# First feed-forward stage of a two-block transformer kernel: down projections of feature pairs by seven block products, conv taps of the gate by halves, values kept in the product banks

## The reference, cut to what matters

```
u = causal_depthwise_conv(h @ w_up, conv_w, conv_b)      # 3 taps along the positions
gate, val = split(u)                                     # 2816 columns each
y = (gelu(gate) * val) @ w_down
```

## Time and profile before

| | us |
|---|---|
| median of 3 runs | 2795.94 (2794.5 to 2797.42) |
| profiled execution | 2795.87 |
| its span, first to last instruction | 2794.1 |
| PE busy | 2703.7 (97%) |
| DVE busy | 1700.7 (61%) |
| POOL busy | 1650.8 (59%) |
| ACT busy | 906.3 (32%) |
| mean granted TensorE clock | 0.992 of full speed |

### The profile page before, as it was taken

How to read it: one execution, slowest core, us unless ns; L and a number is a source line. 1 busy time by engine, 2 the same in 40 slices (tenths; PEclk the granted TensorE clock), 3 DMA queues, 4 the chain that set the end, 5 groups by cost and what they waited for, 6 DMA issues and landing times.

```text
span 2794.1 us, 38419 instructions
## 1 busy us (share of the span) xinstructions
PE 2703.7 (97%) x13018; PEld 2160.0 (77%) x13018; DVE 1700.7 (61%) x2404; ACT 906.3 (32%) x1776; POOL 1650.8 (59%) x1253
## 2 busy tenths in 40 slices
PE   8999999898999999999999999989999999999998
PEld 5777777676878888887788887767787878888887
DVE  6666687738467777777734302475546356766667
ACT  5544444535211111114413113555233222122222
POOL 4555411455988777766533243212356998888874
PEclk9999999999999999999999999999999999999999
DMA  4322321034111211224411243212435111111134
GB/s 146 102 84 84 98 91 54 16 136 149 66 46 48 66 45 48 65 68 169 172 55 46 82 143 106 78 59 88 161 107 173 38 57 56 54 56 53 56 122 142
DMA packets 83012, 243.36 MB, mean 87 GB/s; under 512 B 7839, under 2 KB 11712, under 8 KB 82500
## 3 DMA queue, kind: packets, MB, share of 16 engines
q1 hardware_dynamic: 60800, 183.79, 20.7%
q10 hardware_dynamic: 22084, 57.86, 5.8%
HBM read 206.48 MB, written 32.52 MB: 86 GB/s over the span
## 4 chain that ended last, share of the span: by engine, by line
PE 80%; DVE 9%; POOL 5%; ACT 3%; issue 2%; DMA 0%; POOLq 0%; ACTq 0%; DVEq 0%; SPq 0%
PE ps L1069 14%; PE ps L1071 14%; PE ps L1070 14%; PE ps L1391 4%; PE ps L1392 3%; PE ps L1393 3%; PE ps L1443 3%; PE ps L1445 3%; PE ps L1444 3%; PE ps L1160 2%; PE ps L1483 2%; PE ps L1485 2%; PE ps L1484 2%; PE ps L1176 2%; POOL arena L868 1%
## 5 line engine op out<-in xcount | busy, mean ns | idle before, releaser
L800 POOL CAST wh<-raw 128x1024 fp32r<-128x1024 f32 x173 | 185.1, 1070 | 826.8 <-PE ps L1071 777.4
L1069 PE MATMUL ps<-hh,wh 128*128 128x512 f32 x1456 | 600.2, 412 | 15.5 <-DVE hl L2861 10.9
L1071 PE MATMUL ps<-hh,wl 128*128 128x512 f32 x1456 | 572.2, 393 | 0.0
L1070 PE MATMUL ps<-hl,wh 128*128 128x512 f32 x1456 | 571.5, 392 | 0.0
L802 POOL TENSOR_TENSOR wl<-raw,wh 128x1024 fp32r<-128x1024 f32 x173 | 417.9, 2416 | 13.9
L1069 PEld LDWEIGHTS ps<-hh,wh 128*128 128x128 f32 x1456 | 275.7, 189 | 87.6 <-issue 15.5
L1071 PEld LDWEIGHTS ps<-hh,wl 128*128 128x128 f32 x1456 | 275.4, 189 | 59.8
L1070 PEld LDWEIGHTS ps<-hl,wh 128*128 128x128 f32 x1456 | 276.2, 190 | 52.2 <-issue 3.4
L3154 DVE TENSOR_TENSOR arena<-ps,arena 128x512 f32<-128x512 f32 x288 | 195.8, 692 | 23.6 <-PE ps L1071 23.6
L894 POOL TENSOR_TENSOR wl<-raw,wh 128x512 fp32r<-128x512 f32 x136 | 189.7, 1394 | 10.9
L1069 PE MATMUL ps<-gated,wh 128*128 128x512 f32 (+1 forms) x464 | 178.9, 386 | 2.9 <-DVE gated L2952 2.6
(11 more groups left out here) (401 smaller groups left out, 5922.0 us busy)
## 6 DMA issues: line engine op xcount, KB each, us to landing
raw<-weights SPq DMA_DIRECT2D x226, 512.0 KB, 3.6
arena<-w_ada SPq DMA_DIRECT2D x48, 512.0 KB, 3.7
raw<-weights SPq DMA_DIRECT2D x88, 256.0 KB, 2.6
arena<-gate_scratch ACTq DMA_DIRECT2D x20, 512.0 KB, 4.3
arena<-x_t ACTq DMA_DIRECT2D x1, 4096.0 KB, 14.1
x_scratch<-arena ACTq DMA_DIRECT2D x2, 2048.0 KB, 8.9
arena<-x_scratch SPq DMA_DIRECT2D x2, 2048.0 KB, 9.7
gate_scratch<-arena ACTq DMA_DIRECT2D x16, 256.0 KB, 2.2
```

The source lines that it names most:

```text
L800: pool.tensor_copy(wh[:, s], raw[:, r]).then_inc(Z.wt_hi, 1)
L1069: pe.matmul(out, wh[:, slot, w], xh, start=start, stop=False)
L1070: pe.matmul(out, wh[:, slot, w], xl, start=False, stop=False)
L1071: return pe.matmul(out, wl[:, slot, w], xh, start=False, stop=stop)
```

## The change

The first stage gets the pair scheme of the second: `pair_up`, `pair_down`, `pair_unit`, `pair_loads`, `cast`, `first_blocks`, `second_blocks` and `pair_sums` take `use` as an argument, and the single-feature loops (`st_splits`, `st_chunks`, `st_step1`) go. The weights of the first stage are laid out in pairs too. New is the DVE and ACT order for a stage with a conv: the taps of gate go half by half, each half reading its own bank (the two columns that cross the halves are kept in a small copy, `EDGE`, and added by `edge_taps`); the value is convolved and multiplied half by half, half 1 first, and each product goes into bank 2 or 3. In the tail the down of the last pair takes the place of the single downs of feature 19. The diff's core:

```diff
@@ PE
-                st_up(0, 0)
-                st_down(0, 0)
-                if use == 0:
-                    st_up(1, 1)
-                    st_down(1, 1)
-                    with pe.Fori(0, (ST_N - 2) // 2) as i:
-                        for u in range(2):
-                            st_up(i * 2 + (2 + u), u)
-                            st_down(i * 2 + (2 + u), u)
-                    pe.sem_inc(Z.chunk_done, ST_CHUNKS)
+                st_up()
+                st_down()
+                pair_up(0, 1, 1, 1)
+                pair_up(1, 0, 2, 2)
+                pair_down(0, 3, 3)
+                pair_up(1, 1, 4, 4)
...
                 def pair_up(pair, second, k, ks):
+                    if use:
+                        pe.wait_ge(Z.g_lin, n * 2 + (ST_DONE - 1))
+                    else:
+                        pe.wait_ge(R.lin_first, gate_lin(n, 0))
+                        pe.wait_ge(Z.g_cv, gate_taps_done(n, 2 - 6))
+                    pair_block(k, ks, 0, 0, A_BLOCK[use][0, 0], True)
...
+                        pe.wait_ge(Z.g_cv, gate_taps_done(n, 4 - 6))
+                    pair_block(k, ks, 1, 1, S_BLOCK[use][2], True)
...
                     if second:
-                        pe.wait_ge(Z.a_hi, highs(pair, 1))
+                        pe.wait_ge(HIGH_SEM[use], highs(use, pair, 1))
                     else:
-                        pe.wait_ge(Z.a_lo, lows(pair, 6 - PAIR_LOWS))
-                    pair_block(k, ks, 3, 3, S_BLOCK[1][1], True)
+                        pe.wait_ge(LOW_SEM[use], lows(use, pair, 6 - PAIR_LOWS))
+                    pair_block(k, ks, 3, 3, S_BLOCK[use][1], True)
...
@@ PE, tail
                 half_tile(tail, 0, 0)
-                if use:
-                    pe.wait_ge(Z.a_lo, lows(PAIRS - 1, 8))
-                else:
-                    pe.wait_ge(val_free[0], NL * val_free[1])
+                pe.wait_ge(LOW_SEM[use], lows(use, PAIRS - 1, 8))
                 half_tile(tail, 0, 1)
...
-                if use:
-                    pair_down(PAIRS - 1, LAST_DOWN, LAST_DOWN)
-                    pe.sem_inc(Z.chunk_done, 2)
-                else:
-                    half_down(0, 0, range(KT))
+                pair_down(PAIRS - 1, LAST_DOWN, LAST_DOWN)
+                pe.sem_inc(Z.chunk_done, 2)
                 half_down(1, 0, low)
...
                 if use == 0:
-                    for features in (range(3), range(3, 4)):
-                        half_down(0, 1, features)
-                        half_down(1, 1, features)
+                    half_down(1, 1, low)
                     running_mean(5, 0)
                     half_down(2, 1, low)
-                    half_down(0, 1, high)
                     half_down(1, 1, high)
                     half_down(2, 1, high)
@@ ACT, one up of the new order (the first of a pair)
+            def first_up1(m, prev, k, ks):
+                before, n = prev * 2 + 1, m * 2
+                value_lin(before, 0)
+                gelu_half(before, 1)
+                pair_copy(0, n, k)
+                product_high(0, before, 1, A22_H, bank(3))
+                cast(0, k, ks, False, 2)
+                cast(0, k + 1, ks + 1, True, 0)
+                product_high(0, before, 2, A12_H, bank(2))
+                sum_high(0, prev, 4, S1_H, S1_F)
+                sum_high(0, prev, 5, S2_H, S2_F)
+                gate_first(n, k)
+                sum_high(0, prev, 7, S4_H, S4_F)
+                cast(0, k + 1, ks + 1, True, 1)
+                gelu_half(n, 0)
+                gate_second(n)
@@ DVE
+            def value_taps(n, half):
+                j, pair = n + ST_FIRST, bank(2, 2)
+                dve.wait_ge(Z.v_lin, n * 2 + (ST_FIRST + 2))
+                for m in range(2):
...
+                    dve.scalar_tensor_tensor(t, pair[:, a - 1 - m:end - 1 - m], conv_col(j, 5 - m), t, ALU.mult, ALU.add).then_inc(Z.v_cv, 1)
+            def gated_half(n, half):
+                t = half_of(half)
+                dve.wait_ge(Z.g_act, n * 2 + (ST_FIRST + 1 + half))
+                dve.wait_ge(Z.v_cv, value_taps_done(n, 2 if half else 4))
+                dve.tensor_tensor(bank(2 + half), ST_VALUE[:, t], ST_GATE[:, t], ALU.mult).then_inc(R.p_prod, 1)
+            def gated_value(n):
+                for half in (1, 0):
+                    value_taps(n, half)
+                    gated_half(n, half)
+            def pair_unit1(n, k, lows_left):
+                first_sums(0, n, k)
+                gate_taps(n, 0, 0)
+                gate_taps(n, 0, 1)
+                second_value(0, n, k)
+                if lows_left is not None:
+                    last_lows(0, lows_left)
+                second_gate(0, n, k)
+                gate_taps(n, 1, 0)
+                first_value(0, n, k)
+                gate_taps(n, 1, 1)
+                edge_taps(n)
+            def pair_step1(m, prev, k):
+                gated_value(prev * 2 + 1)
+                second_blocks(0, prev)
+                pair_unit1(m * 2, k, prev)
+                pair_sums(0, Y1t, prev, k + 1)
+                gated_value(m * 2)
+                first_blocks(0, m)
+                pair_unit1(m * 2 + 1, k + 2, None)
...
+            def last_lows(use, pair):
+                dve.wait_ge(LOW_SEM[use], lows(use, pair, 7))
+                block_low(use, pair, 7, S2_L, S2_F, S2_H)
+                block_low(use, pair, 8, S4_L, S4_F, S4_H)
...
             for u in range(2):
                 unit_taps(1, u, 0)
                 unit_taps(1, u, 1)
                 product1(1, u)
                 unit_low(1, u)
-            dve.wait_ge(Z.dn_free, 4 + 16 * ND)
+            pair_sums(0, Y1t, PAIRS - 1, LAST_DOWN)
```

More of the change, by code:

```diff
@@ L794, in _ @@
+            chunk_range(first, N_CHUNKS)
         @block.gpsimd
@@ L1310, in eight_tiles @@
                             ready(k)
-                        last = product(bank(y_bank(use, f, half)), c % SL, k, x[0][k][:, t], x[1][k][:, t], k == 0, k == KT - 1)
+                        last = product(bank(y_bank(use, f, half)), wt_slot(c), k, x[0][k][:, t], x[1][k][:, t], k == 0, k == KT - 1)
                         if n in (second, second + 3) and k == 3:
@@ L2718, in product_high @@
[L2718 to L2724 removed]
             def first_highs(pair, copy):
[L2727 removed]
+                product_high(1, pair * 2, 1, G1_F, bank(3))
@@ new lines, in first_blocks, with second_blocks @@
+            def first_blocks(use, pair):
+                dve.wait_ge(PROD_SEM[use], prods(use, pair * 2, 2))
+                dve.wait_ge(HIGH_SEM[use], highs(use, pair, 2))
+                block_sum(use, S3_F, 2, G1_F, ALU.subtract)
+                block_low(use, pair, 2, A11_L, bank(2), A11_H)
+                block_low(use, pair, 3, S3_L, S3_F, S3_H)
+            def second_blocks(use, pair):
+                dve.wait_ge(HIGH_SEM[use], highs(use, pair, 4))
+                block_sum(use, S1_F, 3, G1_F, ALU.add)
+                dve.wait_ge(LOW_SEM[use], lows(use, pair, 3))
+                block_sum(use, S2_F, 3, S3_F, ALU.subtract)
+                dve.wait_ge(PROD_SEM[use], prods(use, pair * 2 + 1, 2))
+                block_low(use, pair, 4, A22_L, bank(3), A22_H)
+                dve.wait_ge(HIGH_SEM[use], highs(use, pair, 5))
+                dve.wait_ge(LOW_SEM[use], lows(use, pair, 5))
+                block_sum(use, S4_F, 2, S2_F, ALU.subtract)
+                block_low(use, pair, 5, A12_L, bank(2), A12_H)
+                block_low(use, pair, 6, S1_L, S1_F, S1_H)
@@ L3608, in first_blocks @@
                 gate_half(n, 1)
+                first_value(1, n, k)
                 gate_half(n, 0)
[L3610 to L3635 removed]
@@ L3749, in chunks @@
     return w.reshape(k, P, feature_tiles, P).transpose(2, 1, 0, 3).reshape(feature_tiles, P, k * P)
-def ffn_chunks(gate, value, down):
-    out = 2 * [gate[0], value[0], gate[1], value[1]] + [down[0]]
-    for j in range(2, NL):
-        out += [gate[j], value[j], down[j - 1]]
-    a, b = NL, NL + 1
-    return np.stack(out + 2 * [gate[a], value[a], gate[b], value[b], down[ND], down[a], down[b]])
 def pair_chunks(gate, value, down):
```

947 lines of the change are left out of this document (478 added, 469 removed).

## The result

The changed kernel takes 2839.8 us (median of 4 runs, 2839.1 to 2842.19) against 2796.68 for the kernel before beside it: 1.0155 times as long, 95% interval 1.0137 to 1.0172. The prediction was 2811.5 with a range to 2827.0: the sign was right, the size, +15.6 for a measured +43, was not.

A forecast was written before the change was run, and what follows sets the result against it. PE was taken to set the time while DVE keeps its deadlines. Summed: -18.6 + 16.8 + 5.9 + 1.3 + 3.8 + 1.0 + 5.4 = +15.6 us on 2795.87, so 2811.5; 8 in 10 range 2788 to 2827.

The forecast's parts named there:

- Matmuls removed, with the pair's pace: First stage: 96 down matmuls fewer save 21.8 us, less 3.2 for the pairs' slower matmuls, leaving 18.6 us.
- Block 3's wait for A22_L: First up of each pair: PE waits for DVE's A22_L before block 3, 1.5 us in each of seven pairs.
- Second tile of the tail: Tail: PE waits for A12_L before the value's tile in bank 2, 5.9 us, bounds 4.4 and 8.
- First sum of the last down: Last pair's down: block 1 waits for a sum standing behind unit_low on DVE, 3.8 us.
- Half clock in the tail, over before: Tail: PE's clock drops after the last two stalls, costing 1.3 us for the longer and 1.0 for the shorter.
- Idle time given back later: Waits for the running mean and hl: 24 removed matmuls stood ahead of them, so 5.4 us return as idle time.
- two edge taps of about 0.20: DVE, each first-stage feature: the two taps across the halves cost about 0.20 us each.
- The products' port wait: DVE's gated products beside POOL: 0.5 us extra each, two before A22_L, so 1.0 us per pair; bounds 0 and 1.3 each.
- The second stall: Start of down: S2_L and S4_L make the first down sum late, 0.9 us in each of seven pairs, bounds 0.15 and 1.5.
- A: Rival: DVE is in time everywhere, all deadline stalls in loop and tail vanish, 2782.7 us; chance 0.15.
- B: Rival: no port waits, DVE's products fall between POOL's operations; -0.3 us, 2795.6 us; chance 0.20.
- C: Rival: full port waits on each product and low, 32.1 us in the loop; +33.0, 2828.9 us; chance 0.12.

The follow-up runs named there:

- e0: Changed kernel with each feature's two edge taps left out, semaphore counts kept (two gate columns lack terms): 2812.7 us, 1.0052 of the kernel before.
- e12: Changed kernel with the two edge taps written as three one-column DVE operations, nothing left out: 2816.9 us, 1.0072 of the kernel before.
- e2: Changed kernel with the gated products reading the bank they write instead of the gelu in SBUF (values differ): 2822.9 us, 1.0098 of the kernel before.
- e6: Changed kernel with S2's low half moved ahead of the first sums, S4's left in place: 2833.9 us, 1.0138 of the kernel before.
- e3: Changed kernel with edge taps left out and products taking one source from a bank (values differ): 2807.5 us, 1.0042 of the kernel before.
- e1: Changed kernel with edge taps on DVE reading one SBUF tensor, bias added instead of the column (two columns differ): 2824.8 us, 1.0100 of the kernel before.
- e8b: Changed kernel with two tail edits: banks of second and fourth tiles swapped, last down's first four sums ahead of the fourth tile's value taps: 2835.9 us.
- e4: Changed kernel with the edge taps moved from DVE to ACT as three one-column operations, nothing left out: 2811.1 us, 1.0049 of the kernel before.
- e8_act_tail: Changed kernel with edge taps on ACT as in e4 and both tail edits of e8b: 2808.2 us, 1.0045 of the kernel before.
- e9: e8_act_tail with A22_L written ahead of the second gated product and S2's low half ahead of the first sums: 2809.2 us, 1.0038 of the kernel before.
- e11: e9 with 28 matmuls of unused results in three gaps of the tail: 2800.9 us, 1.0016 of the kernel before.
- e10: Changed kernel with six matmuls of unused results ahead of the A22_L wait in each pair's first up: 2838.9 us, 1.0149 of the kernel before.

## Why the prediction was wrong

The stalls that the prediction named are all there, behind the operations that it named. What failed is the price of one operation in them, and what it left out are the half clock in the loop and the start of the stage. By term of the sum, predicted and measured, the latter from the waits and windows above:

| Term | Predicted | Measured |
|---|---|---|
| Matmuls removed, with the pair's pace | -18.6 | about -14.5 |
| Block 3's wait for A22_L, 7 x | 10.5 | 19.1 |
| First down sum, 7 x | 6.3 | 6.8 |
| Half clock in the loop | 0 | 6.3 |
| Second tile of the tail | 5.9 | 7.6 |
| First sum of the last down | 3.8 | 4.5 |
| Half clock in the tail, over before | 2.3 | 4.6 |
| Start of the stage: gap and half clock | 0 | 4.1 |
| Idle time given back later | 5.4 | 4.8 |
| Sum | +15.6 | +43.3 of 44.0 |

**The step that failed** is "two edge taps of about 0.20" (0.53 for both in the walk). The row that it rests on reads a bank; the new taps read two SBUF tensors beside POOL. The prediction gives the two products such a wait and puts that of the edge taps at nothing, without a reason. But the wait is what is left of POOL's operation, whatever DVE's own width: 1.5 to 1.6 us ahead of A22_L instead of 0.53 for the two. With all that follows from it, at both deadlines, at the start, in the tail and in the clock, that is 27 of the 43 us (e0), and 23 of them are the form alone (e12).

**The products' port wait** was sized at 0.5 each; the median is 1060 ns against 695 with a bank, so 0.37, up to 1.1. By the median that would do for the loop. But the second product before A22_L is no median case: it took 1.72 to 1.79 in all seven pairs, since POOL's two L932, which run back to back, begin just ahead of it each time. e2 put the two products' share of the stall at 1.3 a pair; the prediction had 1.0.

**The second stall** had the right size by luck, with the wrong cause. I put it on S2_L and S4_L (0.75 of 0.9); e6, which moved S2_L and left S4_L where DVE then waits for PE behind it, shows them worth 0.1 to 0.2, and in e0 and e12, where the edge taps between the last gate tap and the first down sum are out or don't wait, the stall is gone with both lows in place.

**Half clock in the loop** was costed at nothing: the sum has it behind the tail's two stalls alone, since they are as long as the 3.07 us of the earlier trace rows. The trace shows it behind gaps of 2.69, 2.64, 2.65 and 2.57 as well, four times 1.4 to 1.6 us.

**The start** wasn't in the sum: down_sums of feature 3 stands on DVE behind the edge taps of the first pair (2.41 us, L1049 on L3263; 0.55 in e0), and half clock behind it costs 1.7.

**The pair's pace.** Between its stalls a pair without half clock takes 58.1 (846.19 to 907.83, less 2.53 and 1.01), not 57.52: 0.6 a pair, 4.1 in all. Two slow first matmuls behind the stalls (0.1 each) explain part of it; the rest is open.

**The tail** went as written, but for its clock: A12_L 7.6 within its bounds (4.4 and 8), the last down 4.5 with 3.8 predicted, half clock 4.6 with 2.3, since the stretches are 9 and 13 matmuls long where the one that the prediction took its price from has some 7, and the matmuls that had stood ahead of the late waits came back as idle time, though at three waits rather than two. Their rows after (as the earlier trace rows):

```profile
1372.17 0.50 PE L1049 MATMUL ps<-gated,wh 128*128 128x512 f32 x1 [2.28 <-DVE arena L3292]
1377.16 1.22 PE L1277 MATMUL ps<-arena,mats 128*128 128x512 f32 x1 [4.02 <-DVE arena L2954]
1393.68 0.51 PE L1049 MATMUL ps<-hh,wh 128*128 128x512 f32 x1 [1.52 <-DVE hl L2986]
```

**The rivals.** A is refuted: no first block of a pair was in time. B's loop was made (e3) and is 0.5 late, as B said. C had 32.1 for the loop's port waits and stalls, and they were 25.9, yet the time passed C's, for the half clock in the loop and the start, which no case contained. The top of the range, 2827, came out too low because all cases shared the same 0.20.

Open: what decides that one gap of 2.6 us brings the clock down and the next doesn't; the 0.6 us of the pace; and the gap of the fourth pair, 3.4 to 3.9 in the changed kernel, e0, e1, e6, e8b and e12, where the others have 1.2 or 2.6, but 1.2 in e4 and e8_act_tail. In the changed kernel its first product took 1.59 us, where it took 0.70 in most; in e2, without that wait, the fourth gap is 1.74, near the others. Why POOL stands otherwise in this pair was not tried.

## What to carry to other kernels

Take an operation's price from a row with the same sources (bank or SBUF) and the same neighbours, not from one of the same width: beside a busy POOL a DVE operation on one column with two SBUF tensors costs what is left of POOL's operation, here 0.64 us on the mean for one column and 0.89 for two, against 0.27. Small additions in front of a deadline are written as one-column operations with a value per partition, or go to ACT. And where an engine with some 10 us of slack in a pair still misses a deadline, moving one operation mostly moves the wait (e8b, e9); what helped here is taking work out of the chain, or keeping PE's clock up in a gap that can't be avoided (e11).

## What the hardware showed that I had not expected

- A DVE operation on one column with two SBUF tensors waits for POOL's operation, an addition or a cast, to end (636 ns on the mean, against 268 for the form with one tensor in the same window of e12); with one tensor of one column it never does (48 times 261 to 274 ns); with one tensor of two columns it does (628).
- In the loop of the changed kernel PE's clock fell to 1.2 GHz behind gaps of 2.69, 2.64, 2.65 and 2.57 us, and not behind those of 2.37, 2.53 and 3.68; in e6 behind that of 3.91 and none of the six of 2.35 to 2.67. Behind the loop's gaps of 0.93 to 1.74 us in e0, e2, e4 and e12 it never did; in e10 it did behind one of 2.06 with six filler matmuls ahead of it. Length alone does not decide.
- Matmuls whose results nobody uses, 28 of them or 6.3 us of PE time in gaps, made the stretch 6.2 us shorter and the kernel 6.2 to 8.3 us faster.
- A one-column operation of ACT takes 0.38 us in the mean where DVE's takes 0.27.
